# Where the modulation chunks of the first block stand: fewer in the attention's heads, more beside its output slots and in the first MLP

## The chip, the core and the metric

The kernel runs on one core of a Trainium2 chip. The metric is the device time of one execution in microseconds (us); lower is better. The engines meant below: TensorE (PE in the profile; its weight loads are PEld), VectorE (DVE), ScalarE (ACT), GpSimd (POOL) and SyncE (SP). Each runs its own stream of instructions in order and waits on semaphores that others raise.

## The reference, cut to what matters

The model is two blocks of two layers each over a sequence of 256 rows and 1024 columns. The change touches the first block alone:

```python
def ada_modulation(c, w, b):
    mod = jax.nn.silu(c) @ w + b
    shift, scale, gate = jnp.split(mod, 3, axis=-1)
...
for i in range(DEPTH):
    shift, scale, gate = ada_modulation(c, ada_w[i, 0], ada_b[i, 0])
    h = x * (1.0 + scale) + shift
    y = windowed_gqa(h, ...)   # i = 0; a recurrent block for i = 1
    x = layer_norm(DN_ALPHA * x + (1.0 + gate) * y, ln_g[i, 0], ln_b[i, 0])
    shift, scale, gate = ada_modulation(c, ada_w[i, 1], ada_b[i, 1])
    y = sq_relu_mlp(x * (1.0 + scale) + shift, mlp_w1[i], mlp_w2[i])
    x = layer_norm(DN_ALPHA * x + (1.0 + gate) * y, ln_g[i, 1], ln_b[i, 1])
```

`c` is one vector of 1024, and `ada_w` holds four matrices of 1024 x 3072, one for each of four sublayers: attention, MLP, recurrence, MLP. The attention has 8 query heads of 128, two key heads, and an output projection.

## The kernel before, in words

All engines' streams are written out by hand, sublayer after sublayer (s = 0 is the attention, s = 1 the first MLP). There is no planner: what stands ahead of what on an engine is the order in the program.

**Weights.** Weights come in slots of 128 x 2048 floats (1 MB). SyncE loads a slot into one of three raw buffers when the low half of the slot three earlier is made. ScalarE rounds it to a high half (`hi_upto`, L1016), and VectorE subtracts to make the low half (`lo_upto`, L1397; the instruction is L1403). Three split buffers exist, so the high half of slot n needs TensorE to be done with slot n - 3. TensorE multiplies high by high, low by high and high by low (L516 to L518). `step(label)` on ScalarE and VectorE splits ahead, up to two slots past the one named. The attention has six input slots and four output slots; then the MLP's slots come in the order w1 0, w1 1, w2 0, w1 2, w2 1, w1 3 and so on. Each slot of 48 narrow or 24 wide matmuls takes TensorE between 5 and 6 us.

**Modulation chunks.** The product of `silu(c)` with the four modulation matrices is not done on TensorE as a matmul of weights, but in 96 chunks of 128 x 1024 floats (512 KB). Chunk q is multiplied on VectorE by a column of c and added to one of three accumulators (`ada_upto(q)`, L1440: all chunks up to q that are not yet done; L1450 for the first of eight, L1453 for the others). Eight chunks make one third (shift, scale or gate) of a sublayer. TensorE then sums the accumulator over the partitions with 8 small matmuls against a column of ones (`ada_reduce(t)`, L609, which waits for chunk 8t + 7), and VectorE turns the sum into columns (`modulation(t)`, L1464). Sum 4 is the scale of the first MLP. The chunks lie in a ring of four buffers: the load of chunk q is issued when chunk q - 4 is used. From chunk 20 on GpSimd issues the loads (`ada_load`, L2049), in order with its other work: chunks 20 to 44, then it waits for the normalized rows of s = 0, loads the bucket table and the bias rows (L2059, L2060), then chunks 45 to 63, and so on.

**The attention's heads.** A loop of 11 steps runs on all engines: in step h the scores of head h (TensorE, L683; VectorE adds the window and takes the maximum, L1548 to L1552), the exponentials of head h - 1 (ScalarE) and their division by the sum (VectorE, L1542), the transposes of head h - 2 (TensorE, L694), the product with the values of head h - 3 (L708), and for each pair of heads the output's high half (ScalarE, L1119) and low half (VectorE, L1558). At the end of each step VectorE calls `ada_upto(29 + h)`.

**The output slots and the norm.** TensorE runs `rows_slot` for output slots 0 and 1 with `ada_reduce(4)` between them, then `rows_tail` for slots 2 and 3, which finishes the first 128 rows first (`y_half`), so that VectorE can start the residual and the norm (`norm`, L1600; first step L1574) while TensorE works on. VectorE does, for output slot i, `step`, at i = 1 `modulation(4)`, and `ada_upto(40 + i)`.

**The first MLP.** For each i VectorE does `step` of the w1 slot, the squared ReLU and its low half, `ada_upto(45 + 10 * (i + 1) // 3)`, and `step` of the w2 slot (L1656). The call at i = 0 reaches chunk 48.

Of the kernel before, what the change touches and what calls it, by code (L numbers as in the profile page):

```python
# [101 lines left out]
def build(nc, I, C, out, counts, n_sub):  # L102
# [5 lines left out]
    with ctx:  # L108
# [173 lines left out]
        def inc(name, key=None, by=1):  # L282

            level[name] = level.get(name, 0) + by
            made[(name, key)] = level[name]
            return sem(name), by

        def past(name, key=None):

            return sem(name), known.get((name, key), 1)  # L290
# [113 lines left out]
        for s in range(4, 10):  # L404
            i = s - 4
# [40 lines left out]
        def ada_at(q):  # L446

            return AD0[:, q, :] if q < N_FIRST else ADR[:, q % NADR, :]
# [46 lines left out]
        def _(pe):  # L495
# [3 lines left out]
            def topen(label, consumer):  # L499

                t = tiles[0]
                tiles[0] += 1
                owner[t] = (label, consumer)
                made[("tile", label)] = t
                if t >= NTB:
                    pe.wait_ge(*past("free_" + owner[t - NTB][1], owner[t - NTB][0]))
                return TB[:, t % NTB, :]

            def open_slot(label):
                n = number[label]  # L510
                pe.wait_ge(*past("lo_ready", n))
                return n, slot_view(WHI, n, NSPL), slot_view(WLO, n, NSPL)

            def mm3(o, a, b, c, d, first, last):

                pe.matmul(o, a, c, start=first, stop=False)  # L516
                pe.matmul(o, a, d, start=False, stop=False)  # L517
                return pe.matmul(o, b, c, start=False, stop=last)  # L518
# [28 lines left out]
            def rows_slot(label, lh, ll, k0, first):  # L547

                n, wh, wl = open_slot(label)
                for t in range(NT):  # L550
                    for kk in range(2):
                        xa, xb = lh(k0 + kk)[:, t * P:(t + 1) * P], ll(k0 + kk)[:, t * P:(t + 1) * P]
                        for h in range(2):
                            ins = mm3(Y[:, t, h * 512:(h + 1) * 512], xa, xb, wh[:, kk, h * 512:(h + 1) * 512],
                                      wl[:, kk, h * 512:(h + 1) * 512], first and kk == 0, False)
                ins.then_inc(*inc("rows_done", label))

            def rows_part(label, lh, ll, k0, first, last, t, h):

                n, wh, wl = open_slot(label)  # L560
                for kk in range(2):
                    xa, xb = lh(k0 + kk)[:, t * P:(t + 1) * P], ll(k0 + kk)[:, t * P:(t + 1) * P]
                    ins = mm3(Y[:, t, h * 512:(h + 1) * 512], xa, xb, wh[:, kk, h * 512:(h + 1) * 512],
                              wl[:, kk, h * 512:(h + 1) * 512], first and kk == 0, last and kk == 1)
                return ins

            def rows_tail(s, a, b, b_ready):

                la, lb = a[0], b[0]
                for h in range(2):  # L570
                    rows_part(*a, False, False, 0, h)
                b_ready()
                for h in range(2):
                    ins = rows_part(*b, False, True, 0, h)
                ins.then_inc(*inc("y_half", s))
                rows_part(*a, False, False, 1, 0)
                rows_part(*b, False, True, 1, 0).then_inc(*inc("y_third", s))
                rows_part(*a, False, False, 1, 1).then_inc(*inc("rows_done", la))
                if s + 1 < n_sub:
                    prep(s + 1, 0)  # L580
                rows_part(*b, False, True, 1, 1).then_inc(*inc("rows_done", lb))
                if s + 1 < n_sub:
                    keep_busy(s, b, WARM_ROWS)
                    prep(s + 1, 1)
                    keep_busy(s, b, WARM_XT)

            def keep_busy(s, slot, n):

                pe.wait_ge(*past("y_free", (s, 0)))
                x = OH[:, 0, :] if is_mix(s) else slot[1](slot[3])  # L590
                for _ in range(n):
                    pe.matmul(Y[:, 0, 0:S], x[:, 0:P], x, start=True, stop=True)
# [16 lines left out]
            def ada_reduce(t):  # L609

                if 8 * t >= n_ada:
                    return
                pe.wait_ge(*past("ada_used", 8 * t + 7))
                bank = topen(("ada", t), "D")
                for j in range(8):
                    ins = pe.matmul(bank[:, j:j + 1], ACC[:, t % 3, j * P:(j + 1) * P], ONES[:, 0:1], start=True, stop=True)
                ins.then_inc(*inc("tile_done", ("ada", t)))
# [12 lines left out]
            def prep(s, t):  # L630

                if s > 0:
                    pe.wait_ge(*past(f"xn_ready{t}", (s - 1, t)))
                else:
                    pe.wait_ge(*past("x_in"))
                for g in range(2):
                    bank = topen(("xt", s, t, g), "AD"[g * t])
                    for kk in range(4):
                        k = 4 * g + kk
                        ins = pe.transpose(bank[:, kk * P:(kk + 1) * P], XN[:, t, k * P:(k + 1) * P], IDN[:, :])  # L640
                    ins.then_inc(*inc("tile_done", ("xt", s, t, g)))
# [85 lines left out]
                    gate_rows(0)  # L727
            pe.wait_ge(*past("free_D", ("o", 3)))
            for i in range(2):
                if i == 1:  # L730
                    ada_reduce(4)
                rows_slot((0, "out", i), lambda k: OH[:, k, :], lambda k: OL[:, k, :], 2 * i, i == 0)
            rows_tail(0, *(((0, "out", i), lambda k: OH[:, k, :], lambda k: OL[:, k, :], 2 * i) for i in (2, 3)), lambda: None)

            def mlp(s):
# [658 lines left out]
        def _(dve):  # L1394
# [21 lines left out]
            def chain(ins):  # L1416
                link(dve, ins, "dve_chain")
# [22 lines left out]
            def ada_upto(q):  # L1440

                while chunk[0] <= min(q, n_ada - 1):
                    m = chunk[0]
                    chunk[0] += 1
                    t, kc = divmod(m, KC)
                    dve.wait_ge(*past(f"ada_first{m}" if m < N_FIRST else f"ada_in{m % NADR}" if m < 20 else f"ada_next{m % NADR}", m))
                    if kc == 0:
                        if t >= 3:
                            dve.wait_ge(*past("tile_done", ("ada", t - 3)))
                        ins = dve.tensor_scalar(ACC[:, t % 3, :], ada_at(m), CC[:, kc:kc + 1], None, ALU.mult)  # L1450
                    else:
                        dve.wait_ge(*past("ada_used", m - 1))
                        ins = dve.scalar_tensor_tensor(ACC[:, t % 3, :], ada_at(m), CC[:, kc:kc + 1], ACC[:, t % 3, :],  # L1453
                                                       ALU.mult, ALU.add)
                    ins.then_inc(*inc("ada_used", m))
# [88 lines left out]
            for h in range(NH1 + 3):  # L1544
                if h < NH1:
                    bank = tile(("sc", h))
                    w = slice(2 * h, 2 * h + 2)
                    dve.scalar_tensor_tensor(PR[:, h, :, :].rearrange("p a b -> p (a b)"), bank, HD1 ** -0.5, WIN[:, :],  # L1548
                                                 ALU.mult, ALU.add).then_inc(*inc("free_D", ("sc", h)))
                    dve.wait_ge(*past("free_D", ("sc", h)))  # L1550
                    chain(dve.tensor_reduce(AT1[:, 0, w], PR[:, h, :, :], AX.X, ALU.max))
                    dve.tensor_scalar(AT1[:, 1, w], AT1[:, 0, w], SNK[:, h:h + 1], -1.0, ALU.max, ALU.mult).then_inc(*inc("neg_max", h))  # L1552
                if 1 <= h <= NH1:
                    norm1(h - 1)
                if h >= 4 and h % 2 == 0:
                    i = (h - 4) // 2
                    dve.wait_ge(*past("oh_ready", (0, i)))
                    dve.tensor_tensor(OL[:, 2 * i:2 * i + 2, :], pair_of(y_bank(2 + i % 2)), OH[:, 2 * i:2 * i + 2, :].bitcast(F32),  # L1558
                                          ALU.subtract).then_inc(*inc("free_D", ("o", i)))
                if h in (2, 5):  # L1560
                    modulation({2: 2, 5: 3}[h])
                ada_upto(29 + h)
            for i in range(4):
                step((0, "out", i))
                if i == 1:
                    modulation(4)
                ada_upto(40 + i)

            def residual(s, t, c0, c1):

# [614 lines left out]
```

## Time and profile before

| what | us |
|---|---|
| median of 3 runs | 2298.21 |
| lowest and highest run | 2297.90, 2304.68 |
| the profiled execution's own time | 2302.26 |
| its span, first to last instruction | 2300.5 |
| TensorE busy | 2172.3 |
| VectorE busy | 1565.8 |
| ScalarE busy | 1130.4 |
| GpSimd busy | 328.7 |
| VectorE in the chunks of L1453 (74 from the ring) | 99.8 |

The profile is of one execution. The span leaves out what lies before the first and after the last instruction, 1.8 us here. Busy times overlap, so they don't add up to the span; an engine's idle time costs something only where the chain of work that ends last runs through it. The stretch that the change touches lies between about 94 us (first head) and 190 us (second weight slot of the first MLP).

### The profile page before, as it was taken

How to read it: one execution, taken by the hardware profiler on the slowest of the kernel's cores; microseconds unless marked ns; L12 is line 12 of the kernel's file. 1: busy time of each engine (PE TensorE's matmuls, PEld its weight loads, DVE VectorE, ACT ScalarE, POOL GpSimd, SP SyncE). 2: the span in 40 equal slices, each digit the busy share in tenths (PEclk: the TensorE clock that was granted, in tenths of full speed). 3: DMA queues.
4: the chain of work that ended last, by engine and by line, in shares of the span. 5: the costliest groups of instructions: out<-in, count | busy, mean ns of one | idle time of the engine just before them, and what ended most of it. 6: DMA issues, size and time to landing. Idle time of an engine off the chain costs nothing.

```text
span 2300.5 us, 35892 instructions
## 1 busy us (share of the span) xinstructions
PE 2172.3 (94%) x15144; PEld 2003.1 (87%) x15144; DVE 1565.8 (68%) x1870; ACT 1130.4 (49%) x1513; POOL 328.7 (14%) x281
## 2 busy tenths in 40 slices
PE   4889999986999999999999999999999999999998
PEld 3768998975899899999899889999999988988997
DVE  6878887598655745569865674465456995657445
ACT  2344434587444533456664453444345667445432
POOL 2112324011020210030011130012003000212000
PEclk9899999988999999999999999999999999999999
DMA  9749894333465465665432455546565544235552
GB/s 343 238 149 327 303 340 143 114 85 102 164 202 183 154 212 183 165 188 148 120 114 71 144 185 184 183 148 222 188 182 170 153 123 129 74 113 179 194 192 92
DMA packets 304068, 397.00 MB, mean 173 GB/s; under 512 B 47103, under 2 KB 262777, under 8 KB 303908
## 3 DMA queue, kind: packets, MB, share of 16 engines
q1 hardware_dynamic: 285440, 336.75, 45.6%
q0 software_dynamic: 17488, 57.63, 8.0%
q8 instruction: 120, 1.97, 0.4%
q10 hardware_dynamic: 980, 0.32, 0.1%
q14 instruction: 40, 0.33, 0.1%
HBM read 393.60 MB, written 1.07 MB: 172 GB/s over the span
## 4 chain that ended last, share of the span: by engine, by line
PE 72%; DVE 18%; ACT 5%; issue 3%; DMA 1%; SPq 1%; POOL 0%; DVEq 0%; ACTq 0%; POOLq 0%
PE tiles L516 15%; PE tiles L517 15%; PE tiles L518 15%; PE y_rows L516 6%; PE y_rows L517 6%; PE y_rows L518 6%; DVE weights_lo L1403 4%; PE tiles L912 3%; DVE ada_acc L1453 2%; ACT weights_hi L1026 1%; DVE rnn_r L1732 1%; DMA weights_raw<-in_attn_w_in_dram 1%; PE tiles L918 1%; DVE rnn_conv_out L1701 1%; PE tiles L640 1%
## 5 line engine op out<-in xcount | busy, mean ns | idle before, releaser
L1403 DVE TENSOR_TENSOR weights_lo<-weights_raw,weights_hi 128x2048 fp32r<-128x2048 f32 (+2 forms) x316 | 765.9, 2431 | 443.6 <-ACT weights_hi L1026 442.9
L516 PE MATMUL tiles<-xt_hi,weights_hi 128*128 128x256 f32 (+1 forms) x3200 | 914.2, 286 | 16.1 <-DVE xt_lo L1504 9.4
L517 PE MATMUL tiles<-xt_lo,weights_hi 128*128 128x256 f32 (+1 forms) x3200 | 908.2, 284 | 0.0
L518 PE MATMUL tiles<-xt_hi,weights_lo 128*128 128x256 f32 (+1 forms) x3200 | 908.1, 284 | 0.0
L1026 ACT ACTIVATE weights_hi<-weights_raw 128x2048 fp32r<-128x2048 f32 (+2 forms) x316 | 592.6, 1879 | 222.6 <-PE y_rows L518 163.4
L516 PEld LDWEIGHTS tiles<-xt_hi,weights_hi 128*128 128x128 f32 (+1 forms) x3200 | 609.4, 190 | 32.3 <-issue 24.2
L517 PEld LDWEIGHTS tiles<-xt_lo,weights_hi 128*128 128x128 f32 (+1 forms) x3200 | 609.7, 191 | 2.7
L518 PEld LDWEIGHTS tiles<-xt_hi,weights_lo 128*128 128x128 f32 (+1 forms) x3200 | 609.5, 190 | 0.0
L516 PE MATMUL y_rows<-weights_hi,hid_hi 128*128 128x512 f32 x608 | 238.8, 393 | 1.2 <-DVE weights_lo L1403 1.2
L517 PE MATMUL y_rows<-weights_lo,hid_hi 128*128 128x512 f32 x608 | 237.3, 390 | 0.0
L518 PE MATMUL y_rows<-weights_hi,hid_lo 128*128 128x512 f32 x608 | 236.7, 389 | 0.0
L2006 POOL TENSOR_TENSOR x_scaled<-x_rows,ln_gb_rows 128x1024 f32<-128x1024 f32 x18 | 57.7, 3204 | 795.3 <-DVE xt_lo L1504 731.0
L1030 ACT ACTIVATE hid_act<-tiles 128x512 f32<-128x512 f32 x76 | 45.4, 598 | 244.2 <-PE tiles L518 244.1
L518 PEld LDWEIGHTS y_rows<-weights_hi,hid_lo 128*128 128x128 f32 x608 | 114.2, 188 | 24.3
L516 PEld LDWEIGHTS y_rows<-weights_hi,hid_hi 128*128 128x128 f32 x608 | 114.4, 188 | 24.0 <-issue 2.3
L517 PEld LDWEIGHTS y_rows<-weights_lo,hid_hi 128*128 128x128 f32 x608 | 114.5, 188 | 21.1
L1126 ACT ACTIVATE hid_hi<-hid_val 128x512 fp32r<-128x512 f32 x44 | 27.8, 632 | 192.8 <-DVE hid_val L1682 192.8
L1453 DVE SCALAR_TENSOR_TENSOR ada_acc<-ada_ring,c_cols,ada_acc 128x1024 f32<-128x1024 f32 x74 | 99.8, 1348 | 5.6 <-DMA ada_ring<-in_ada_w_dram 0.5
L516 PE MATMUL tiles<-ot_hi,weights_hi 128*128 128x256 f32 x256 | 75.7, 296 | 5.8 <-DVE ot_lo L1943 5.8
L1628 DVE TENSOR_TENSOR hid_lo<-hid_val,hid_hi 128x512 fp32r<-128x512 f32 x76 | 56.7, 746 | 32.0 <-ACT hid_hi L1126 30.8
L517 PE MATMUL tiles<-ot_lo,weights_hi 128*128 128x256 f32 x256 | 74.2, 290 | 0.0
L518 PE MATMUL tiles<-ot_hi,weights_lo 128*128 128x256 f32 x256 | 74.2, 290 | 0.0
(363 smaller groups left out, 2718.6 us busy)
## 6 DMA issues: line engine op xcount, KB each, us to landing
weights_raw<-in_ffn_w_dram SPq DMA_DIRECT2D x132, 1024.0 KB, 5.0
weights_raw<-in_mlp_w_dram SPq DMA_DIRECT2D x64, 1024.0 KB, 6.1
weights_raw<-in_w_in_dram SPq DMA_DIRECT2D x52, 1024.0 KB, 5.2
ada_ring<-in_ada_w_dram POOLq DMA_DIRECT2D x76, 512.0 KB, 5.3
weights_raw<-in_rnn_w_in_dram SPq DMA_DIRECT2D x16, 768.0 KB, 4.6
weights_raw<-in_w_in_dram SPq DMA_DIRECT2D x32, 256.0 KB, 4.2
weights_raw<-in_w_branch_a_dram SPq DMA_DIRECT2D x32, 256.0 KB, 5.0
weights_raw<-in_w_branch_b_dram SPq DMA_DIRECT2D x8, 1024.0 KB, 5.3
```

The costliest lines, as they stand in the source:

```text
L516: pe.matmul(o, a, c, start=first, stop=False)
L517: pe.matmul(o, a, d, start=False, stop=False)
L518: return pe.matmul(o, b, c, start=False, stop=last)
L640: ins = pe.transpose(bank[:, kk * P:(kk + 1) * P], XN[:, t, k * P:(k + 1) * P], IDN[:, :])
L912: ins = pe.matmul(bank[:, j * P:(j + 1) * P], lhs(j), rhs(j), start=True, stop=True)
L1026: act.activation(slot_view(WHI, m, NSPL), slot_view(RAW, m, NRAW), ACT.Copy).then_inc(*inc("hi_ready", m))
L1030: act.activation(dst, src, func, **kw).then_inc(*inc("free_A", label))
L1126: act.activation(HH[:, i % 2, :], src[:, i % 2, :], func).then_inc(*inc("hh_ready", (s, i)))
L1403: dve.tensor_tensor(slot_view(WLO, m, NSPL), slot_view(RAW, m, NRAW), slot_view(WHI, m, NSPL).bitcast(F32), ALU.subtract).then_inc(*inc("l ...
L1453: ins = dve.scalar_tensor_tensor(ACC[:, t % 3, :], ada_at(m), CC[:, kc:kc + 1], ACC[:, t % 3, :], ALU.mult, ALU.add)
L1628: dve.tensor_tensor(HL[:, i % 2, :], VB[:, i % 2, :], HH[:, i % 2, :].bitcast(F32), ALU.subtract).then_inc(*inc("hid_ready", (s, i)))
L2006: chain(pool.tensor_tensor(XS[:, t, :], XN[:, t, :], GB[:, 0, :], ALU.mult))
```

## The change

TensorE's `ada_reduce(4)` moves from between output slots 0 and 1 to behind slot 1. VectorE does one chunk in every second step of the heads and no longer in every step (`29 + h // 2`, up to chunk 34); then chunks up to 36 at output slot 0 and up to 39 at slot 1, and `modulation(4)` at slot 2. The calls in the MLP are as they were, so that the first of them now starts at chunk 40, where it started at chunk 44.

```diff
--- before.py
+++ after.py
@@ -727,9 +727,8 @@
                     gate_rows(0)
             pe.wait_ge(*past("free_D", ("o", 3)))
             for i in range(2):
-                if i == 1:
-                    ada_reduce(4)
                 rows_slot((0, "out", i), lambda k: OH[:, k, :], lambda k: OL[:, k, :], 2 * i, i == 0)
+            ada_reduce(4)
             rows_tail(0, *(((0, "out", i), lambda k: OH[:, k, :], lambda k: OL[:, k, :], 2 * i) for i in (2, 3)), lambda: None)
 
             def mlp(s):
@@ -1559,12 +1558,12 @@
                                           ALU.subtract).then_inc(*inc("free_D", ("o", i)))
                 if h in (2, 5):
                     modulation({2: 2, 5: 3}[h])
-                ada_upto(29 + h)
+                ada_upto(29 + h // 2)
             for i in range(4):
                 step((0, "out", i))
-                if i == 1:
+                ada_upto(36 + 3 * min(i, 1))
+                if i == 2:
                     modulation(4)
-                ada_upto(40 + i)
 
             def residual(s, t, c0, c1):
```

## Rows read from the trace of the kernel before

**Rows 1.** The page, busy time: engine, us busy, share, instructions.
```profile
PE 2172.3 (94%) x15144; PEld 2003.1 (87%) x15144; DVE 1565.8 (68%) x1870; ACT 1130.4 (49%) x1513; POOL 328.7 (14%) x281
```

**Rows 2.** Timeline of VectorE, heads: start, us, engine, line, op, out<-in, count, [idle before].
```profile
109.83 0.69 DVE L1548 SCALAR_TENSOR_TENSOR probs<-tiles,window 128x512 f32<-128x512 f32 x1 [0.23 <-PE tiles L683]
...
112.34 0.75 DVE L1450 TENSOR_SCALAR ada_acc<-ada_ring,c_cols 128x1024 f32<-128x1024 f32 x1
...
121.19 0.68 DVE L1548 SCALAR_TENSOR_TENSOR probs<-tiles,window 128x512 f32<-128x512 f32 x1
...
127.98 1.28 DVE L1453 SCALAR_TENSOR_TENSOR ada_acc<-ada_ring,c_cols,ada_acc 128x1024 f32<-128x1024 f32 x1
...
131.53 0.69 DVE L1558 TENSOR_TENSOR ot_lo<-y_rows,ot_hi 128x512 fp32r<-128x512 f32 x1 [1.35 <-ACT ot_hi L1119]
...
134.72 0.68 DVE L1558 TENSOR_TENSOR ot_lo<-y_rows,ot_hi 128x512 fp32r<-128x512 f32 x1
```

**Rows 3.** Timeline of TensorE, heads and output slots.
```profile
111.68 1.03 PE L683 MATMUL tiles<-k_t,q_t 128*128 128x256 f32 x4
...
119.50 1.11 PE L683 MATMUL tiles<-k_t,q_t 128*128 128x256 f32 x4
...
128.12 1.03 PE L694 MATMUL y_rows<-ident,probs 128*128 128x128 f32 x4 [2.77 <-DVE probs L1542]
...
135.46 0.50 PE L516 MATMUL y_rows<-weights_hi,ot_hi 128*128 128x512 f32 x1 [1.92 <-DVE ot_lo L1558]
...
141.03 1.84 PE L616 MATMUL tiles<-ones,ada_acc 128*128 128x1 f32 x16
142.73 0.49 PE L516 MATMUL y_rows<-weights_hi,ot_hi 128*128 128x512 f32 x1
```

**Rows 4.** Timeline of VectorE, output slots and the norm's first step.
```profile
143.23 2.29 DVE L1403 TENSOR_TENSOR weights_lo<-weights_raw,weights_hi 128x2048 fp32r<-128x2048 f32 x1 [3.77 <-ACT weights_hi L1026]
...
152.73 2.67 DVE L1453 SCALAR_TENSOR_TENSOR ada_acc<-ada_ring,c_cols,ada_acc 128x1024 f32<-128x1024 f32 x2
155.32 1.22 DVE L1574 TENSOR_TENSOR x_rows<-y_rows,gate_rows 128x1024 f32<-128x1024 f32 x1
```

**Rows 5.** Timeline of VectorE, first slot of the MLP.
```profile
178.41 5.44 DVE L1453 SCALAR_TENSOR_TENSOR ada_acc<-ada_ring,c_cols,ada_acc 128x1024 f32<-128x1024 f32 x4
185.04 0.75 DVE L1450 TENSOR_SCALAR ada_acc<-ada_ring,c_cols 128x1024 f32<-128x1024 f32 x1 [1.19 <-DMA ada_ring<-in_ada_w_dram]
185.71 2.28 DVE L1403 TENSOR_TENSOR weights_lo<-weights_raw,weights_hi 128x2048 fp32r<-128x2048 f32 x1
```

**Rows 6.** Timeline of TensorE at slot w1 2.
```profile
188.05 0.39 PE L516 MATMUL tiles<-xt_hi,weights_hi 128*128 128x256 f32 x1 [1.15 <-DVE weights_lo L1403]
```

**Rows 7.** Timeline of GpSimd: DMA issues.
```profile
167.36 0.56 POOL L2059 DMA_DIRECT2D bucket_hot<-table_bucket_hot_dram  x1 [27.08 <-DVE x_rows L1595]
...
179.98 0.53 POOL L2053 DMA_DIRECT2D ada_ring<-in_ada_w_dram  x1 [9.50 <-DVE ada_acc L1453]
```

**Rows 8.** The chunk buffers from 90 to 215 us: time from issue to landing.
```profile
DMA to landing us min/median/max: 3.7/5.0/9.2
```

**Rows 9.** Stretches of TensorE: length, busy (instructions), granted clock, DMA share, GB/s.
```profile
158.00:160.70 2.70, 0.00 (x0) 1.00 0.00 0
447.40:449.20 1.80, 0.00 (x0) 0.97 0.00 0
449.60:455.50 5.90, 5.67 (x21) 0.50 0.17 48
495.00:496.90 1.90, 0.00 (x1) 1.00 0.01 2
497.30:503.60 6.30, 6.26 (x15) 0.50 0.24 55
1975.00:1977.60 2.60, 0.00 (x0) 1.00 0.00 0
1978.20:1981.60 3.40, 3.40 (x19) 0.51 0.13 36
```

## The prediction, made before the changed kernel was run

> **What bounds the kernel now.** I read the page's busy line first, then the timelines of VectorE and TensorE from the first attention's heads to the second weight slot of the first MLP, then GpSimd's timeline, the landing times of the modulation chunks, and the granted clock. The busy line shows TensorE at 94% of the span [rows 1]: a delay of a VectorE step costs time only where TensorE waits for it. The timelines show three such places. In the heads VectorE works nearly without a break and TensorE waits for its probabilities and for its last low half [rows 2, 3]. In the layer norm TensorE waits for the rows: the norm's first step stands at 155.32, right behind two chunks that started at 152.73 [rows 4]. In the MLP VectorE runs chunks until 185.7 before it makes the low half of the slot "w1 2", and TensorE idles 1.15 us until that is done, at 188.05 [rows 5, 6]. That third place decides the forecast: what the change puts ahead of that low half has no cover left.
>
> Where the chunks stand: the heads hold chunks 28 to 39 before and 28 to 34 after (`29 + h // 2`). The output slots hold 40 to 43 before; after, the first holds 35 and 36, the second 37 to 39, the other two none. The next `ada_upto(45 + 10 * (i + 1) // 3)` reaches 48 at i = 0, so w1 0 gets 44 to 48 before (five) and 40 to 48 after (nine). Nothing is added or removed in all, only moved.
>
> **Heads: five chunks less.** At 1.28 us each (0.75 for the first of a third) that is about 6 us of VectorE, but most of it meets another limit. After the chunk of h = 1 VectorE waits for TensorE anyway: scores of head 3 come at 109.83 behind TensorE [rows 2]. The chunk at 112.34 goes, 0.67 from start to start, but scores 4 (TensorE 111.68 + 1.03 = 112.71) start VectorE at 112.75, not 113.01: 0.3 gained. The chunk of h = 5 goes too, but scores 6 are ready at 119.50 + 1.11 = 120.61: VectorE goes on at 120.65, not 121.19: 0.5 gained. At h = 6 the chunk is now chunk 32, the first of a third, 0.5 shorter: 1.06 gained by h = 7. So probabilities 6, which released TensorE at 128.12 [rows 3], come about 1.1 earlier, and the chunk of 127.98 goes too. From there the chain runs over TensorE and ScalarE to the low half of heads 4 and 5 (131.53, after 1.35 of waiting), 1.0 earlier; the last low half (134.72) stood behind two chunks and comes 1.5 earlier, and with it the first output slot: 133.95 for 135.46 [rows 2, 3]. Gain 1.5; bounds 1.0, and 3.0 if the shorter idle time before 128.12 spares TensorE the slower clock.
>
> **Output slots: a new wait.** With the start at 133.95, VectorE does chunk 34 (to 135.0), the low half of the third output slot (2.2 as that at 185.71, to 137.2), chunks 35 and 36 (to 139.9). The next low half needs the first slot's end; it stood at 143.23, 7.77 behind the slot's start [rows 3, 4], so now at 141.7 to 143.95. Then chunks 37, 38, 39: two at 1.39 from start to start (the four of [rows 5]: (5.44 - 1.28) / 3) and one of 1.28, to 148.05. TensorE, which no longer does its 16 reductions of chunk sum 4 between the slots, has done both by 133.95 + 2 x 5.5 = 144.95 and now waits at `ada_reduce(4)` for chunk 39: 3.1 us. Behind that wait on TensorE stands the whole tail, and behind the tail the norm. The reduction itself (1.84) only changes place [rows 3]. Tail start: 149.75 for 148.25, so 1.5 later. But before, the half that the norm waits for was done at 148.25 + 5.5 = 153.8 and VectorE came only at 155.32 because of chunks 42 and 43 [rows 4]; these are gone, and it starts when the half is done, at 155.4. Heads, wait and norm together: +0.1. Bounds of the wait: 2.5, and 4.5 if chunk 39, loaded after chunk 35 at about 138.8, lands after the longest time shown (9.2, so 148.0 for a start at 146.7) [rows 8].
>
> **MLP, w1 0: nine chunks for five.** In the old times, all shifted alike: VectorE starts at 178.41, needs 5.44 for chunks 44 to 47, waits 1.19 for chunk 48, and starts the low half at 185.71 [rows 5]. After, chunks 40 to 43 take 0.85 (0.75 and the 0.1 between dependent chunks) + 3 x 1.39, to 183.4, from data that is there. Chunk 44 goes into the place of 40, and GpSimd can issue its load only after 40 is used, 0.29 behind its end (179.98 stood so behind 178.41 + 1.28): 179.45 [rows 5, 7]. Before, chunk 44's load went out in the output slots, and 45 to 47 right after the norm. GpSimd's queue is in order, so the bucket table's and bias rows' loads, which stood at 167.36, now stand behind 44's issue, and 45 behind them: 45 at 181.5, 46 at 182.2, 47 at 183.6. TensorE wants that table only after w1 3, over 15 us later. A load issued at 179.98 was there for 185.04: 5.06 [rows 5, 7]. Chunk 44 is thus used at 184.5, 45 at 186.6, 46 at 188.0, 47 at 189.4; 48, issued 0.29 after 44 is used (186.1), comes at 191.3 and is done by about 192.1. The low half follows, done at 194.4 for 187.99. TensorE gets w1 2 at 194.45: +6.4. The bounds: 3.9 if no load is late (0.85 + 7 x 1.39 + 0.67 = 11.2 for the 7.3 of before), 8.5 if each of the two rounds of loads (40 to 44 to 48) takes 1 us more. I take 6.4, since the median landing time of the region is 5.0 [rows 8]. No other work of TensorE can slip in, as its stream is in order: w1 2, w2 1, w1 3 all stand behind the wait. VectorE itself is busy to 216 without waiting for TensorE, so nothing of this is given back.
>
> The Trainium skill ("DMA: Bandwidth & Descriptors", section on the anatomy of one DMA on the gpsimd path) gives 2.0 us plus the bytes at 436 per ns; for 512 KB that makes 3.2 us, an estimate, and this step would cost the 3.9 of the lower bound. The loads here show 5.0 in the median, beside weight loads, so the trace speaks against it.
>
> **The clock.** TensorE would stand idle 7.5 us before w1 2 (186.9 to 194.45) and 3.1 us before the reduction. After the idle time around 447.4 to 449.2 it granted 0.50 for 5.9 us of work (1.2 GHz for 2.4), after 495.0 to 496.9 0.50 for 6.3 us, after 1975.0 to 1977.6 0.51 for 3.4 us; after 158.0 to 160.7 it kept 1.00 [rows 9]. At half clock t us of work do what t/2 did, so one drop costs 1.7 to 3.1, taken 2.5. For the 7.5 us I take it as sure; for the 3.1 us as likely, as in three of these four stretches: 2.5 more, as the tail and so the half that the norm waits for are that much later. The Trainium skill ("TensorE: Matmul & The Clock Gate", Part 1) says that this warm-up is worth under 1% of a span and should not be fitted, since it varies from run to run. Each drop is 0.1% here; I keep the term because the whole effect is of that size.
>
> **Sum.** Profiled execution 2302.26 (span 2300.5) + 0.1 + 2.5 (clock in the tail) + 6.4 + 2.5 (clock in w1 2) = 2302.26 + 11.5 = 2313.8. That execution lies 4.05 above the median of the runs, 2298.21, so 2298.21 + 11.5 = 2309.7.
>
> **Rivals.**
> A, the tail keeps its clock (the stretch at 158 did): +9.0, 2307.2. For it: dense matmuls on both sides there as here. Chance 0.20.
> B, the loads keep up: w1 0 costs 3.9 and not 6.4, so +9.0 with both drops, +6.5 with one: 2304.7 to 2307.2. Against it: VectorE waited 1.19 for chunk 48 although 44 to 47 were there [rows 5]. Chance 0.10. This is what the DMA page's formula would bring.
> C, the clock holds at both places: 0.1 + 6.4 = +6.5, or +5.0 with the 3.0 in the heads: 2303.2 to 2304.7. Against it: an idle time twice as long as any in [rows 9]. Chance 0.10.
> D, faster: the heads hang on VectorE throughout and give back all five chunks, 5 x 1.28 = 6.4, while w1 0 costs nothing. It decides if TensorE's scores of heads 3, 4 and 6 come earlier as well, once VectorE's steps do, and if the nine chunks end before TensorE needs w1 2. 2298.2 - 6.4 = 2291.8. For it: VectorE's idle times in the heads are small. Against it: 0.23 behind TensorE at 109.83 [rows 2] and the 1.15 at 188.05 [rows 6]. Chance 0.05.
> E, more than said: late loads at both places (4.5 for 3.1, 8.5 for 6.4) with both drops, 11.5 + 1.4 + 2.1 = +15.0, 2313.2. Chance 0.05.
>
> **Chances.** Forecast 0.50, A 0.20, B 0.10, C 0.10, D 0.05, E 0.05. What this kernel's measurement can tell from no change is about 0.3%, 6.9 us. Forecast, A, E and half of B lie above it (0.80), C and the other half of B below (0.15), D is faster (0.05). The range 2302.5 to 2314.5 leaves out D, the low end of C and the high end of E. Within it the likeliest case spans 2307.5 to 2313 (two clock terms of 1.7 to 3.1, loads 1 either way).
>
> **What would show it.** In the changed trace: output slot 0 starts about 1.5 earlier; TensorE's matmuls of `ada_reduce` for sum 4 stand behind the second slot with about 3 us of idle time released by VectorE's chunk; the norm's first VectorE step has no chunk right before it; VectorE waits for loads of chunks 44, 45 and 48 in w1 0; TensorE's first matmul of w1 2 shows about 7.5 us idle behind a low half, and granted clock 0.5 after it. Wrong would be: TensorE idle before w1 2 of under 3 us, or the first output slot over 4 us earlier.

## The result and the profile after

The changed kernel takes 2312.81 us (median of 4 runs, 2308.59 to 2314.35) against 2299.11 us (4 runs, 2297.90 to 2304.68). The ratio is 1.0054, 95% interval 1.0041 to 1.0067: slower by 9.4 to 15.4 us. Forecast were 2309.7 us and +11.5 us. The profiled execution of the changed kernel is its fastest, 2308.59 us (span 2306.8), 6.3 above the one of before. Its busy line is as good as unchanged; the same work stands in other places:

```profile
PE 2173.4 (94%) x15144; PEld 2002.7 (87%) x15144; DVE 1568.7 (68%) x1870; ACT 1129.4 (49%) x1513; POOL 334.2 (14%) x281
```

The timeline of VectorE in the heads (start, us, engine, line; in brackets the idle time before it and what ended it) answers to [rows 2]:

```profile
112.00 0.69 DVE L1547 SCALAR_TENSOR_TENSOR probs<-tiles,window 128x512 f32<-128x512 f32 x1 [1.18 <-PE tiles L683]
...
119.98 0.69 DVE L1547 SCALAR_TENSOR_TENSOR probs<-tiles,window 128x512 f32<-128x512 f32 x1 [0.87 <-PE tiles L683]
...
128.57 0.69 DVE L1557 TENSOR_TENSOR ot_lo<-y_rows,ot_hi 128x512 fp32r<-128x512 f32 x1 [0.80 <-ACT ot_hi L1118]
...
130.97 0.69 DVE L1557 TENSOR_TENSOR ot_lo<-y_rows,ot_hi 128x512 fp32r<-128x512 f32 x1 [0.52 <-ACT ot_hi L1118]
```

and that of TensorE, through the output slots to the second weight slot of the MLP, to [rows 3, 6]:

```profile
126.38 0.66 PE L694 MATMUL y_rows<-ident,probs 128*128 128x128 f32 x4 [2.23 <-DVE probs L1541]
131.71 0.50 PE L516 MATMUL y_rows<-weights_hi,ot_hi 128*128 128x512 f32 x1 [1.41 <-DVE ot_lo L1557]
145.84 3.58 PE L616 MATMUL tiles<-ones,ada_acc 128*128 128x1 f32 x16 [2.93 <-DVE ada_acc L1452]
...
195.12 0.58 PE L516 MATMUL tiles<-xt_hi,weights_hi 128*128 128x256 f32 x1 [7.03 <-DVE weights_lo L1402]
203.14 1.84 PE L616 MATMUL tiles<-ones,ada_acc 128*128 128x1 f32 x16
```

In the heads VectorE now waits for TensorE at heads 4 and 6 (1.18 and 0.87): the gap that two chunks filled. From VectorE's first score step to the first output slot it takes 131.71 - 95.16 = 36.55 us, against 135.46 - 96.76 = 38.70 before: 2.15 gained. Another 96.76 - 95.16 = 1.6 us of the earlier start lie ahead of the heads, where nothing was edited; they are no gain of the change. Then TensorE waits 2.93 us for chunk 39 before its chunk sum, which takes 3.58 us where it took 1.84 [rows 3]: the granted clock, shown below, has fallen. VectorE's norm no longer stands behind chunks but waits for TensorE, which answers to [rows 4]:

```profile
141.72 4.06 DVE L1452 SCALAR_TENSOR_TENSOR ada_acc<-ada_ring,c_cols,ada_acc 128x1024 f32<-128x1024 f32 x3
...
156.51 1.23 DVE L1573 TENSOR_TENSOR x_rows<-y_rows,gate_rows 128x1024 f32<-128x1024 f32 x1 [6.09 <-PE y_rows L518]
```

From the first output slot to the norm: 156.51 - 131.71 = 24.80 us, before 155.32 - 135.46 = 19.86. In w1 0 ([rows 5]) VectorE works on chunks from 179.61 to 192.8, with a wait for a load in the middle, that of chunk 44. The load of chunk 48 it doesn't wait for:

```profile
179.61 0.75 DVE L1449 TENSOR_SCALAR ada_acc<-ada_ring,c_cols 128x1024 f32<-128x1024 f32 x1
180.47 4.06 DVE L1452 SCALAR_TENSOR_TENSOR ada_acc<-ada_ring,c_cols,ada_acc 128x1024 f32<-128x1024 f32 x3
186.73 5.45 DVE L1452 SCALAR_TENSOR_TENSOR ada_acc<-ada_ring,c_cols,ada_acc 128x1024 f32<-128x1024 f32 x4 [2.20 <-DMA ada_ring<-in_ada_w_dram]
192.12 0.75 DVE L1449 TENSOR_SCALAR ada_acc<-ada_ring,c_cols 128x1024 f32<-128x1024 f32 x1
192.79 2.28 DVE L1402 TENSOR_TENSOR weights_lo<-weights_raw,weights_hi 128x2048 fp32r<-128x2048 f32 x1
```

GpSimd shows why ([rows 7]): the load of chunk 44 is issued only at 180.66, behind the use of chunk 40, and the two small loads stand between it and that of chunk 45.

```profile
180.66 0.53 POOL L2052 DMA_DIRECT2D ada_ring<-in_ada_w_dram  x1 [34.05 <-DVE ada_acc L1449]
181.18 0.56 POOL L2058 DMA_DIRECT2D bucket_hot<-table_bucket_hot_dram  x1
181.72 0.54 POOL L2059 DMA_DIRECT2D rel_bias<-in_rel_bias_dram  x1
182.29 0.10 POOL L2060 MEMSET rel_bias<- 1x16 f32 x1
182.69 0.56 POOL L2052 DMA_DIRECT2D ada_ring<-in_ada_w_dram  x1 [0.30 <-POOL rel_bias L2060]
```

From issue to landing the load of chunk 44 (issued at 180.66) and that of chunk 48 (issued at 188.31) took:

```profile
DMA to landing us min/median/max: 6.0/6.0/6.0
...
DMA to landing us min/median/max: 3.8/3.8/3.8
```

So chunk 48 landed at 192.1, just as VectorE was done with chunk 47.

The low half for w1 2 ends at 195.07, and TensorE has idled 7.03 us. The granted clock in two stretches, behind the wait in the output slots and behind this one (columns as in [rows 9]):

```profile
145.90:152.20 6.30, 6.30 (x23) 0.50 0.94 357
195.20:200.90 5.70, 5.70 (x30) 0.57 0.95 355
```

The cleanest measure is the time between the norms' first steps, since each stretch holds one sublayer. For the first MLP it is 372.64 - 156.51 = 216.13 us, against 362.70 - 155.32 = 207.38: +8.75. From the first score step of the heads to the norm behind the first MLP, the whole stretch that the edits lie in, it is 372.64 - 95.16 = 277.48 us against 362.70 - 96.76 = 265.94: +11.5. By the clock of the trace that norm comes 372.64 - 362.70 = 9.9 us later, because of the 1.6 us ahead of the heads. All later stretches agree within 0.3 us but for two, which hold the two mixers of the model's second part (it follows the layers that the reference above shows, and the change leaves its code alone): 366.1 and 364.8 us here, 366.9 twice before. Some 3 us come back there in this execution. The repeats below tell what that is.

### The profile page after: what moved, and what is told of

Same layout as the page of the kernel before. It is cut to its first block, busy times and chain, and to the rows that moved or that the text cites. A ratio compares the mean times of both kernels' runs of the same rounds, so it can differ in the third digit from the quotient of the medians.

```text
span 2306.8 us, 35894 instructions
## 1 busy us (share of the span) xinstructions
PE 2173.4 (94%) x15144; PEld 2002.7 (87%) x15144; DVE 1568.7 (68%) x1870; ACT 1129.4 (49%) x1513; POOL 334.2 (14%) x281
## 3 DMA queue, kind: packets, MB, share of 16 engines
q8 instruction: 120, 1.97, 0.3%
HBM read 393.60 MB, written 1.07 MB: 171 GB/s over the span
## 4 chain that ended last, share of the span: by engine, by line
PE 74%; DVE 15%; ACT 5%; issue 2%; DMA 2%; SPq 1%; POOL 0%; DVEq 0%; ACTq 0%; POOLq 0%
PE tiles L516 16%; PE tiles L517 15%; PE tiles L518 15%; PE y_rows L516 6%; PE y_rows L517 6%; PE y_rows L518 6%; DVE weights_lo L1402 3%; PE tiles L911 2%; ACT weights_hi L1025 1%; DVE ada_acc L1452 1%; DMA weights_raw<-in_attn_w_in_dram 1%; DVE rnn_r L1731 1%; PE tiles L640 1%; DMA ada_ring<-in_ada_w_dram 1%; PE tiles L616 1%
## 5 line engine op out<-in xcount | busy, mean ns | idle before, releaser
L1125 ACT ACTIVATE hid_hi<-hid_val 128x512 fp32r<-128x512 f32 x44 | 27.8, 632 | 192.8 <-DVE hid_val L1681 192.8
L2052 POOL DMA_DIRECT2D ada_ring<-in_ada_w_dram x76 | 40.5, 532 | 250.6 <-DVE ada_acc L1452 168.1
```

The source lines that it names most:

```text
L1125: act.activation(HH[:, i % 2, :], src[:, i % 2, :], func).then_inc(*inc("hh_ready", (s, i)))
L2052: pool.dma_start(ada_at(q), ada_src(q)).then_inc(*inc(f"ada_next{q % NADR}", q, 16))
```

## The experiments

The theory: the cost sits before w1 2 (nine chunks, the loads of the last five late) and in the clock's falls; the output slots give back what the heads gain. The main rival: the wait in the output slots carries it, and the MLP gives its part back later. Times are ratios to the kernel before with their 95% intervals, and norm to norm for the MLP. The kernel before was run beside each series: its median was 2301.07 us (27 runs) beside e1, e2, e3 and e7, and 2302.47 us (24 runs) beside e5, e6, e9 and e10.

**e1: the four chunks back beside the output slots.**

```diff
                 if i == 2:
                     modulation(4)
+                if i >= 2:
+                    ada_upto(40 + i)
```

> The changed kernel, with chunks 40 to 43 back beside output slots 2 and 3, so that w1 0 gets five chunks again (44 to 48). Theory (the cost sits before w1 2: nine chunks, the last five behind late loads, and the clock that falls): TensorE's idle time before w1 2 goes back to about 1.2 us, the stretch from the norm to the second chunk sum in the MLP is as long as in the kernel before, and the whole is within 4 us of the kernel before (0 to +4: the wait of about 3 us before chunk sum 4 and its clock stay, the heads give 1.5 back, the norm starts late behind chunks again). Rival (the output slots carry the cost: chunk sum 4 and the tail): the time stays near the changed kernel's, +9 us or more.

Measured: 1.0001 (0.9992 to 1.0011), 2299.93 us. The MLP takes 364.83 - 157.38 = 207.45 us, as before (207.38), and TensorE's idle time before w1 2 is back to 1.07. The wait and the slow sum in the output slots are still there:

```profile
146.59 3.03 PE L616 MATMUL tiles<-ones,ada_acc 128*128 128x1 f32 x16 [2.93 <-DVE ada_acc L1452]
...
190.06 0.39 PE L516 MATMUL tiles<-xt_hi,weights_hi 128*128 128x256 f32 x1 [1.07 <-DVE weights_lo L1402]
```

The rival falls. Heads and output slots without the MLP's part cost nothing that can be told in the whole (-1.8 to +2.5 us). By the stages they cost something: from the first score step to the MLP's norm it is 364.83 - 95.66 = 269.17 us, which is 3.2 more than in the first profile before and 1.1 more than in the second (r1 below).

**e2: only the MLP's part.**

```diff
                 if i == 1:
                     modulation(4)
-                ada_upto(40 + i)
```

> The kernel before, with one edit: chunks 40 to 43 are taken from the output slots, heads and chunk sum 4 stay as they were. So w1 0 gets nine chunks. Theory: the norm starts 1.4 us earlier, TensorE idles about 7 us before w1 2, granted clock 0.5 behind it for some 5 us: +6.4 + 2.5 - 1.4 = +7.5 us over the kernel before (6 to 9). Rival (output slots and heads): within 2 us of the kernel before.

Measured: 1.0028 (1.0017 to 1.0039), +6.4 us, 2306.66 us. First output slot to norm: 153.02 - 134.53 = 18.49, which is 1.37 less than before; the MLP takes 369.15 - 153.02 = 216.13, 8.75 more. The sum is +7.4. TensorE:

```profile
192.54 0.58 PE L516 MATMUL tiles<-xt_hi,weights_hi 128*128 128x256 f32 x1 [7.92 <-DVE weights_lo L1403]
201.01 1.84 PE L616 MATMUL tiles<-ones,ada_acc 128*128 128x1 f32 x16
```

**e3: both waits filled with matmuls.**

```diff
+                if t == 4:
+                    bank = topen(("ada", t), "D")
+                    filler(bank, OH[:, 0, :], 22)
                 pe.wait_ge(*past("ada_used", 8 * t + 7))
...
+                if label == (1, "w1", 2):
+                    bank = topen(label, consumer)
+                    filler(bank, xh[:, 0, :], 54)
                 n, wh, wl = open_slot(label)
```

> The changed kernel, with matmuls whose result is thrown away filling both of TensorE's waits: 22 of 256 columns ahead of the wait for chunk sum 4, 54 ahead of the slot w1 2 (0.127 us each, 2.8 and 6.9 us). The waits stay as long as they are. If the clock's fall is a cost of its own, the granted clock stays 1.0 behind both and the kernel is 4 to 6 us faster than the changed one (2.5 to 3 for each). If the clock costs nothing (rival: TensorE waits for VectorE again later anyway), it is within 1 us of the changed one.

Measured: 1.0027 (1.0018 to 1.0037), 2307.68 us; the changed kernel had 1.0054. TensorE and its clock:

```profile
142.79 2.79 PE L615 MATMUL tiles<-ot_hi 128*128 128x256 f32 x22
145.88 1.95 PE L628 MATMUL tiles<-ones,ada_acc 128*128 128x1 f32 x16 [0.30 <-DVE ada_acc L1464]
...
186.57 6.63 PE L615 MATMUL tiles<-xt_hi 128*128 128x256 f32 x54
194.78 0.38 PE L516 MATMUL tiles<-xt_hi,weights_hi 128*128 128x256 f32 x1 [1.59 <-DVE weights_lo L1414]
```

```profile
145.90:149.00 3.10, 3.10 (x22) 1.00 0.97 353
149.60:152.60 3.00, 3.00 (x9) 0.52 1.04 385
194.80:200.00 5.20, 5.20 (x43) 1.00 0.99 399
```

Before w1 2 the filler does what was expected: the clock stays at 1.00, and the MLP takes 369.71 - 155.13 = 214.58, 1.55 less, although the low half itself came about 1 us later behind the norm here (39.65 for 38.61). In the output slots it does so for the chunk sum (1.95 us, clock 1.00), but from 149.1 the clock is down all the same, to 152.6. First slot to norm: 155.13 - 131.77 = 23.36, 1.44 less. In all 3.0 us by the two stretches, where 4 to 6 were expected; the medians are 5 us apart, in separate series. So the clock is a cost of its own, shown before w1 2, where it stayed up. In the output slots the filler kept it up for the sum alone; its fall behind the sum wasn't prevented by filling the idle time.

**e4: VectorE's work in w1 0 cut, loads as they are.**

```diff
+                        w = 8 if 41 <= m <= 43 else D
...
-                        ins = dve.scalar_tensor_tensor(ACC[:, t % 3, :], ada_at(m), CC[:, kc:kc + 1], ACC[:, t % 3, :],
-                                                       ALU.mult, ALU.add)
+                        ins = dve.scalar_tensor_tensor(ACC[:, t % 3, 0:w], ada_at(m)[:, 0:w], CC[:, kc:kc + 1],
+                                                       ACC[:, t % 3, 0:w], ALU.mult, ALU.add)
```

> The changed kernel, with chunks 41 to 43 multiplied over 8 of their 1024 columns only (the sum of these three chunks is left out of the other columns), loads and waits as they are. It parts VectorE's work from the loads' lateness in w1 0. By VectorE's work alone (rival) TensorE's idle time before w1 2 shrinks by the work taken away, 3 x 1.2 = 3.6 us, to about 3.4. By the chain of loads (chunk 44 can be loaded only after 40 is used, 48 only after 44), VectorE waits for chunk 44 instead, about 5 us in place of 2.2, and the idle time shrinks by 1 us at most, to 6 or more.

Measured: one run, 2313.2 us (the kernel before on the same chip: 2302.84). VectorE's work shrinks by 3.2 us (0.89 for 4.06 in three chunks) and its wait for chunk 44 grows to 5.54; TensorE idles longer than in the changed kernel, and the MLP takes 374.62 - 157.87 = 216.75 us, no less than with the work in place:

```profile
181.82 0.89 DVE L1453 SCALAR_TENSOR_TENSOR ada_acc<-ada_ring,c_cols,ada_acc 128x8 f32<-128x8 f32 x3
188.26 1.28 DVE L1453 SCALAR_TENSOR_TENSOR ada_acc<-ada_ring,c_cols,ada_acc 128x1024 f32<-128x1024 f32 x1 [5.54 <-DMA ada_ring<-in_ada_w_dram]
190.16 4.06 DVE L1453 SCALAR_TENSOR_TENSOR ada_acc<-ada_ring,c_cols,ada_acc 128x1024 f32<-128x1024 f32 x3 [0.62 <-DMA ada_ring<-in_ada_w_dram]
194.51 0.75 DVE L1449 TENSOR_SCALAR ada_acc<-ada_ring,c_cols 128x1024 f32<-128x1024 f32 x1 [0.28 <-DMA ada_ring<-in_ada_w_dram]
```

```profile
197.52 0.58 PE L516 MATMUL tiles<-xt_hi,weights_hi 128*128 128x256 f32 x1 [8.06 <-DVE weights_lo L1402]
```

So the delay up to chunk 44 is set by the load of chunk 44, which waits for the use of chunk 40, and not by the arithmetic on chunks 41 to 43: the rival falls. The second round (44 used, 48 loaded) is less clear-cut. Here VectorE waits 0.28 for chunk 48, in e2 0.64 and in the changed kernel not at all: that load is hidden behind the four chunks from 44 to 47, and the two take about as long. What less arithmetic on these four would bring was not tried.

**e7: the nine chunks spread over the MLP.**

```diff
-                        ada_upto(45 + 10 * (i + 1) // 3)
+                        ada_upto([43, 47, 51, 55, 59, 63, 67][i] if i < 7 else 45 + 10 * (i + 1) // 3)
```

> The changed kernel, with the MLP's chunks spread: w1 0 takes 40 to 43 (data that is there), the next steps four each up to 47, 51, 55, 59, 63, 67, then as before. Theory: no idle time of TensorE before w1 2 (the low half is done at about 7 us behind the first chunk, before TensorE gets there), so 9 to 10 us faster than the changed kernel and within 3 us of the kernel before. Rival (in all too much VectorE work in the MLP, wherever it stands): the idle time moves to a later slot, and less than half of the loss comes back.

Measured: 1.0023 (1.0013 to 1.0033), 2305.06 us. There is no idle time before w1 2 any more. But the MLP takes 369.97 - 157.16 = 212.81, 5.4 more than before and only 3.3 less than with nine at once. 4.14 us stand before slot w2 7 (the expectations of e5 and e9 call it w2 6), behind a step with four chunks and the decay operations (from 271.6 to 275.5):

```profile
266.22 5.44 DVE L1452 SCALAR_TENSOR_TENSOR ada_acc<-ada_ring,c_cols,ada_acc 128x1024 f32<-128x1024 f32 x4
...
275.54 4.48 DVE L1402 TENSOR_TENSOR weights_lo<-weights_raw,weights_hi 128x2048 fp32r<-128x2048 f32 x2
```

```profile
277.97 0.76 PE L516 MATMUL y_rows<-weights_hi,hid_hi 128*128 128x512 f32 x1 [4.14 <-DVE weights_lo L1402]
```

The clock falls twice as well: slot w2 1 takes 203.61 - 196.44 = 7.17 us and w2 7 285.75 - 277.97 = 7.78, where such a slot takes 5.6 in the kernel before. The theory's 9 to 10 us failed. The rival's "less than half comes back" holds in the MLP's stretch (3.3 of 8.75), not in the whole (0.31 of 0.54%); that the idle time moves to a later slot is shown. Room for VectorE is scarce in the whole MLP.

**e9: spread evenly.** As e7, with the list 43, 47, 52, 56, 60, 64, 68, so that step 7 keeps three chunks.

> The changed kernel with the nine chunks spread once more, now so that step 7 of the MLP, which also holds the 4 us of small decay operations, keeps its three chunks: up to 43, 47, 52, 56, 60, 64, 68, then as before. Theory: the 4.1 us of idle time before slot w2 6 of the first spreading come from the fourth chunk there and go, with their drop of the clock; what is left over the kernel before is the wait in the output slots: +0 to +3 us, 3 us or more faster than the first spreading. Rival (the MLP as a whole has no room for four more chunks): the idle time stays, at another slot.

Measured: 1.0012 (1.0002 to 1.0021), 2304.63 us, MLP 212.10. The wait at step 7 is gone, but others have come, before w2 2 and w2 6, as TensorE's timeline shows. The whole is within the +0 to +3 us of the theory (+2.8), but its "3 us faster" than e7 failed: 0.7 in the MLP, some 2.5 by the ratios. In both spreadings the four extra chunks cost some 5 us of the MLP's stretch, and over 3 us of that are falls of the clock (here w2 1 takes 203.92 - 196.75 = 7.17 us and w2 6 272.36 - 265.20 = 7.16).

```profile
211.69 0.47 PE L516 MATMUL y_rows<-weights_hi,hid_hi 128*128 128x512 f32 x1 [1.11 <-DVE weights_lo L1402]
...
265.20 0.47 PE L516 MATMUL y_rows<-weights_hi,hid_hi 128*128 128x512 f32 x1 [2.87 <-DVE weights_lo L1402]
```

**e5: the kernel before, with two chunks less in the tail.**

```diff
-                ada_upto(40 + i)
+                ada_upto(min(40 + i, 41))
...
-                        ada_upto(45 + 10 * (i + 1) // 3)
+                        ada_upto([45, 48, 52, 56, 60, 64, 68][i] if i < 7 else 45 + 10 * (i + 1) // 3)
```

> The kernel before, with chunks 42 and 43 taken from output slots 2 and 3, and the MLP's chunks spread: w1 0 takes 42 to 45, the steps after it up to 48, 52, 56, 60, 64, 68, then as before. Theory: the norm starts when the first half of its rows is done, 1.4 us earlier, and the low half for w1 2 comes about 1.9 us earlier, so that TensorE's 1.15 us before w1 2 go: 2 to 2.5 us faster than the kernel before. Rival (VectorE's stream in the MLP is full, and what w1 0 gives away comes back at a later slot, as with nine chunks spread, where 4.1 us of idle time stood before slot w2 6): within 1 us of the kernel before or slower.

Measured: 0.9982 (0.9973 to 0.9991), 2297.88 us. First slot to norm 152.75 - 134.21 = 18.54, 1.3 less, as expected. The MLP takes 361.06 - 152.75 = 208.31, 0.9 more: the 1.15 before w1 2 went, but 1.75 stand before slot w2 6 (0.46 in the kernel before), and in w2 7 the clock falls (7.09 us for 5.54). So the rival came true in part. The whole is more than the two stretches explain (see the repeats).

**e6 and e10: the chunk sum in the tail.** The list of e5 in the MLP, and

```diff
-            ada_reduce(4)
-            rows_tail(0, ... for i in (2, 3)), lambda: None)
+            rows_tail(0, ... for i in (2, 3)), lambda: ada_reduce(4))
...
                 if i == 2:
                     modulation(4)
+                    ada_upto(41)
```

e10 has `ada_upto(40)` there and 44 as the first of the list.

> The changed kernel, with the sum of the chunks' third 4 moved into the tail, behind its first 12 matmuls (2.7 us later), chunks 40 and 41 beside output slot 2, and the MLP's chunks spread (w1 0 takes 42 to 45, then up to 48, 52, 56, 60, 64, 68). Theory: TensorE's wait before that sum falls from 2.9 to under 0.5 us and the clock stays up; the heads' 2 us stay gained; the norm starts at about 19.6 us behind the first output slot (19.9 in the kernel before, 24.8 in the changed one); no idle time before w1 2. In all 3 to 4 us faster than the kernel before. Rival (the MLP gives it back at a later slot): within 1 us of it.

> As the version with the sum in the tail, but only chunk 40 beside output slot 2, and w1 0 takes 41 to 44. Theory: the norm starts up to 1.2 us earlier than there (VectorE is free when the half is done), nothing else moves: 0 to 1 us faster than it. Rival: TensorE's half is done later than VectorE's chunk 41 anyway: the same time.

Measured: e6 0.9972 (0.9961 to 0.9983), 2295.70 us; e10 0.9969 (0.9957 to 0.9980), 2295.61 us. TensorE and VectorE in e6:

```profile
133.19 0.50 PE L516 MATMUL y_rows<-weights_hi,ot_hi 128*128 128x512 f32 x1 [1.41 <-DVE ot_lo L1556]
147.29 1.95 PE L616 MATMUL tiles<-ones,ada_acc 128*128 128x1 f32 x16 [0.21 <-DVE ada_acc L1451]
```

```profile
151.22 1.28 DVE L1451 SCALAR_TENSOR_TENSOR ada_acc<-ada_ring,c_cols,ada_acc 128x1024 f32<-128x1024 f32 x1
152.42 1.22 DVE L1573 TENSOR_TENSOR x_rows<-y_rows,gate_rows 128x1024 f32<-128x1024 f32 x1
```

The wait is 0.21 instead of 2.93, the sum takes 1.95, and the norm starts 19.23 behind the first slot. The MLP takes 206.88 (e10: 208.22, with one fall of the clock at 269 to 272 where e6 has none). e10's norm starts 18.93 behind the slot, 0.3 of the possible 1.2 earlier, and its whole time is that of e6, as its rival said. Both beat both kernels, the one before by 0.3%. From the first score step to the first norm it is 56.38 us in e6 and 55.78 in e10, against 57.18 in e5, which has the full heads, and 58.56 in the kernel before: the thinned heads are worth keeping, with the sum where it waits only 0.21 us and without the extra chunks in w1 0. The other part of the 0.3% lies in the mixers (next).

**r1, r2: both kernels once more.**

> The kernel before once more, for a second profiled execution. What belongs to the program repeats: 19.9 us from the first output slot to the norm, 207.4 us from that norm to the next, 1.1 us of idle time before w1 2. The two mixers of the second block (366.9 us from norm to norm in the first profile, 364.8 to 365.6 in several of the experiments) may differ: they have idle times that sit at the edge of the clock's fall. If they do, some 2 us each of the whole are luck of an execution and belong to no edit.

> The changed kernel once more. By the theory 24.8 us from the first output slot to the norm and 216.1 us from norm to norm repeat within 1 us (against 19.9 and 207.4), so that it is 9 to 11 us behind the kernel before at the first MLP's norm, and what differs from its first profile lies in the mixers.

Measured (one run each): 2303.29 and 2312.55 us. First slot to norm: 19.87 and 24.89. MLP: 208.67 (1.3 more than in the first profile; the transposes at its start took 1.97 for 1.09) and 216.61. Idle time before w1 2: 1.07 and 7.61. The mixers take 366.9 us in both, all four times. In e1, e2 and e5 to e10 they take 365.4 to 366.7 and 364.8 to 365.3, in e3 and e4 366.9 again, whatever was edited upstream. So up to 3.5 us of a whole run come or go in the mixers, and no edit here touches them. The traces show where. In each mixer TensorE idles 2.72 to 2.78 us before the same transposes, in all thirteen profiles. Behind that idle time the clock is down in some and stays up in others; here the first mixer of the kernel before and of e1, timeline and clock of each:

```profile
1221.39 3.67 PE L918 MATMUL tiles<-ident,t_inv_t 128*128 128x128 f32 x16 [2.78 <-DVE t_inv_t L1894]
...
1223.49 1.97 PE L917 MATMUL tiles<-ident,t_inv_t 128*128 128x128 f32 x16 [2.78 <-DVE t_inv_t L1895]
...
1221.40:1226.40 5.00, 5.00 (x24) 0.50 0.28 93
1223.50:1228.50 5.00, 5.00 (x45) 1.00 0.31 95
```

Where the granted clock of these five us is 1.00, the mixer takes 364.8 to 365.6 us; where it is 0.50 to 0.73, 366.1 to 367.0. This holds for all 26 of them. Why the clock does the one or the other behind equal idle times, the traces don't show.

With equal mixers the two executions r1 and r2 lie 9.3 us apart. From the first score step to the MLP's norm they take 268.07 and 278.36 us: +10.3, where the first pair of profiles gives +11.5.

## Why the prediction was right, step by step

| term | forecast | shown |
|---|---|---|
| heads, first output slot earlier by | 1.5 | 2.15; with the same course of the clock 1.55 |
| wait before chunk sum 4 | 3.1 | 2.93 (all versions with it: 2.92 to 2.93) |
| norm no longer behind chunks, earlier by | 1.45 | 1.37 (e2), 1.32 (e5); in the changed kernel it waits 6.09 for TensorE |
| clock in sum and tail | 2.5 | about 3.3: sum 3.43 for 1.70 to the next matmul, then 7.24 to the norm for 5.64 in e2 |
| norm to w1 2, longer by | 6.4 | 38.61 - 32.73 = 5.9; second pair 39.21 - 34.01 = 5.2 |
| clock in w1 2 | 2.5 | 203.14 - 195.12 = 8.02 for 5.86: 2.2 |
| first MLP in all, norm to norm | 8.9 | 8.75; second pair 7.9 |
| first score step to the MLP's norm, in all | 11.5 | 11.5; second pair 10.3 |

**The bound** was read rightly: in both profiles before, TensorE idled 1.1 us before w1 2 (1.15 in [rows 6], 1.07 in r1), so the place had no cover, and the stall went through to the end. e1 and e2 show it from both sides: without the MLP's part +0.2 us (-1.8 to 2.5), with it alone +6.4.

**The late loads** were right in kind, and their size came out in part by luck. The load of chunk 44 was issued at 180.66 and used at 186.73, 6.07 behind; [rows 8] gave 5.0, [rows 5, 7] 5.06. The load of chunk 48 took 3.8 (3.9 in r2) where 5.06 was taken. The prediction had VectorE wait for chunks 44, 45 and 48; it waited for 44 alone. One us more in the first round and none of the second round's wait evened out to 5.9 for 6.4. That the load of chunk 44, and not VectorE's work beside it, sets the first round is shown by e4. The Trainium skill ("DMA: Bandwidth & Descriptors", anatomy of one DMA on the gpsimd path) gives an estimate of 3.2 us for such a load. The 6.0 of chunk 44 decides against it where the weight loads run beside it (378 GB/s from 180.7 to 186.7); the 3.8 of chunk 48, where less was under way (234 GB/s from 188.3 to 192.1), comes closer. Rival B had all loads keep up, and chunk 44 did not.

**The clock** fell at both places as forecast, at 1.2 GHz for 6.3 us, and for some 4.9 of the 5.7 us that the second stretch covers (0.57). Rivals A and C are out. The term in the tail was too small by 0.8, since the sum itself runs at the lower level too. e3 shows that the term before w1 2 exists, but also that my reason for a fall was incomplete: I ascribed it to the idle time, and in e3 the clock fell at 149.1 behind 0.30 of idle time. Nor is the length of the idle time enough to tell: the stretches of [rows 9] lie in idle times of 2.27, 2.34, 2.79 and 2.78 us, and behind 2.79 the clock stayed up in the first profile before and fell in r1 (transposes of 1.09 and 1.97 us). In the tail it fell in all six profiles with the wait, behind 2.92 to 2.93 us.

**The heads** gave 0.65 more than forecast, and that is the clock. Behind the idle time at head 6 it fell before (0.53 from 128.1 to 131.0) and stayed at 1.00 here, which the forecast had as its upper bound. In e6, with the same heads as the changed kernel, it fell there as it did before, and the stretch took 133.19 - 96.04 = 37.15 instead of 36.55: 1.55 less than the 38.70 before, as forecast. That the shorter idle time (2.23 for 2.77) spared TensorE the fall isn't shown: in e6 it fell behind 2.24, and in e5 it stayed up behind 2.77.

**What evened out.** In the first pair of profiles the heads gave 0.65 more than forecast, the tail cost 0.8 more and the MLP 0.15 less, so that the sum is met to 0.1. So close a match is luck: the second pair gives 10.3, and the two profiles of each kernel, paired crosswise, give 9.4 and 12.4, since the falls of the clock and the loads differ from execution to execution. The ratio of the runs says 12.4 (9.4 to 15.4). The four runs of the kernel before in it have a median of 2299.11 us, the 51 beside the experiments 2301.07 and 2302.47, and against these the changed kernel's 2312.81 is 11.7 and 10.3 longer. What the whole time adds to the stages is in the mixers, which no step of the prediction looked at.

## What to carry to other kernels

When work is moved off one engine's busy stretch, look first at what stands behind its new place: here a low half for which TensorE already waited 1.1 us, so each microsecond put before it counted in full. With a ring filled on demand, count the rounds of loads beside the work: nine chunks from a ring of four that had stopped being refilled needed two loads one after the other, the first of them 6.0 us, and cutting the arithmetic beside that one gained nothing. And put a small reduction where its last input is there and its result isn't needed yet: 2.7 us later in TensorE's stream, the wait of 2.9 us shrank to 0.2 and the clock stayed up (1.00 from 147.3 to 152.0 in e6).

## What was not expected of the hardware

The granted clock can fall with hardly any idle time before it. In e7, TensorE was busy from 192.0 on, from 194.35 with the 16 one-column matmuls of a chunk sum, with 0.24 us of idle time at 196.4; from 197.3 to 200.3 its clock was at 0.52:

```profile
192.00:194.30 2.30, 2.30 (x21) 1.00 1.04 363
194.30:196.20 1.90, 1.90 (x18) 1.00 0.88 319
197.30:200.30 3.00, 3.00 (x9) 0.52 0.94 328
```

The same stands behind chunk sums in e3 (at 149.1, after 0.30 of idle time), in e9 (197.9, after 0.24), and in e5 and e10 (about 270, after 0.53). Most chunk sums are not followed by it: in the kernel before none of the first MLP's was. Whether the chunk sum has a part in it wasn't tested. What the traces do show is that neither a busy TensorE nor a short idle time is a warrant that the clock stays up.
